# Routing inside the output projection, expert rows added in DRAM by an accumulating DMA, and twelve raw weight pieces

## The reference

```python
x = x + jnp.concatenate([o_diff, o_swa], axis=-1) @ w_out[l]
n2 = rms_norm(x, norm2_g[l])
x = x + hier_moe(n2, ...)          # top group of 4, then top 2 of its 8 experts
return rms_norm(x, final_g)

# in hier_moe, T = 2048 tokens, 32 experts
pg = jax.nn.softmax(xt @ w_rg + b_rg);  p_top, g_idx = lax.top_k(pg, 1)
el = (xt @ w_re + b_re).reshape(T, N_GROUPS, EXPERTS_PER_GROUP)
v2, i2 = lax.top_k(take_along_axis(el, g_idx), 2)
gates = jax.nn.softmax(v2) * p_top
h = jax.nn.silu(xb @ w_gate[e]) * (xb @ w_up[e]);  y = h @ w_down[e]
out = out.at[token].add(y * gate)
```

## Time and profile before

| | us |
|---|---|
| median of 3 runs (2435.26 to 2440.82) | 2435.41 |
| span of the profiled execution | 2437.1 |
| `output_projection`, first residual to last | 1106.88 to 1327.22 |
| `routing`, SP's first issue to the next stage's | 1341.66 to 1405.48 |
| `experts`, first turning of x to last copy of y | 1412.87 to about 2345.8 |
| `combine`, first issue to the end | 2348.89 to 2437.1 |

### The profile page before, as it was taken

The page is one execution under the profiler, slowest core; times in us unless marked ns, Lnnn a source line. Parts: engine busy times, 40 slices in busy tenths (PEclk is TensorE's granted clock), DMA queues, the critical chain, the costliest instruction groups (busy, mean ns, idle before and its releaser), DMA issues. The chain is left out here.

```text
span 2437.1 us, 39765 instructions
## 1 busy us (share of the span) xinstructions
PE 2097.6 (86%) x12636; PEld 1764.5 (72%) x12637; DVE 1347.6 (55%) x2184; ACT 1114.7 (46%) x2349; POOL 427.7 (18%) x568
## 2 busy tenths in 40 slices
PE   5999999779999947969999278999999999999940
PEld 4888888657777737958787267888887888788840
DVE  5333332278888834642332867565467467655537
ACT  4111111167887834642322157555456456645512
POOL 0112111123333432001110300000000000000036
PEclk9999999989999978989999589999999999999975
DMA  6323323341243464333331379777679679877648
GB/s 195 105 89 105 97 91 96 100 141 54 78 138 108 131 168 117 90 91 104 103 103 69 108 251 346 259 271 254 223 267 319 218 256 333 277 248 258 215 150 298
DMA packets 333564, 421.86 MB, mean 173 GB/s; under 512 B 19761, under 2 KB 245681, under 8 KB 333489
## 3 DMA queue, kind: packets, MB, share of 16 engines
q1 hardware_dynamic: 313056, 349.80, 45.1%
q0 software_dynamic: 12672, 46.14, 5.7%
q10 hardware_dynamic: 7760, 24.97, 2.6%
HBM read 321.76 MB, written 99.09 MB: 173 GB/s over the span
## 5 line engine op out<-in xcount | busy, mean ns | idle before, releaser
L56 PE MATMUL proj<-w_in_lo,n1T_hi 128*128 128x512 f32 (+1 forms) x640 | 245.0, 383 | 18.1 <-DVE w_in_lo L257 18.1
L57 PE MATMUL proj<-w_in_hi,n1T_lo 128*128 128x512 f32 (+1 forms) x640 | 239.5, 374 | 0.0
L58 PE MATMUL proj<-w_in_hi,n1T_hi 128*128 128x512 f32 (+1 forms) x640 | 239.3, 374 | 0.0
L525 ACT ACTIVATE prob<-score,nmax 128x512 f32<-128x512 f32 (+3 forms) x344 | 206.5, 608 | 52.0 <-DVE nmax L599 47.5
L1694 DVE TENSOR_TENSOR wg_lo<-raw_pieces,wg_hi 128x1024 fp32r<-128x1024 f32 x124 | 146.9, 1222 | 118.5 <-ACT wg_hi L1662 118.3
L57 PE MATMUL u_ps<-wu_hi,xT_lo 128*128 128x256 f32 x752 | 211.3, 281 | 0.0
L58 PE MATMUL u_ps<-wu_hi,xT_hi 128*128 128x256 f32 x752 | 211.3, 281 | 0.0
L56 PE MATMUL u_ps<-wu_lo,xT_hi 128*128 128x256 f32 x752 | 211.2, 281 | 0.0
L561 POOL TENSOR_SCALAR prob<-prob,scale,lam 128x512 f32<-128x512 f32 (+3 forms) x172 | 147.1, 866 | 241.0 <-DVE scale L615 224.9
L599 DVE TENSOR_REDUCE nmax<-score 128x2 f32<-128x1024 f32 (+3 forms) x172 | 171.5, 997 | 26.6 <-PE score L639 18.0
L56 PE MATMUL y_ps<-wd_lo,hT_hi 128*128 128x512 f32 x376 | 157.8, 420 | 28.5 <-DVE hT_lo L1705 28.1
(11 more groups left out here) (236 smaller groups left out, 5015.8 us busy)
## 6 DMA issues: line engine op xcount, KB each, us to landing
raw_pieces<-in_w_gate SPq DMA_DIRECT2D x128, 512.0 KB, 6.0
raw_pieces<-in_w_up SPq DMA_DIRECT2D x128, 512.0 KB, 6.9
raw_pieces<-in_w_down SPq DMA_DIRECT2D x128, 512.0 KB, 4.8
qk_scratch<-qkT SPq DMA_DIRECT2D x96, 256.0 KB, 2.3
y_scratch<-y ACTq DMA_DIRECT2D x47, 512.0 KB, 6.8
x_sb<-in_x SPq DMA_DIRECT2D x32, 512.0 KB, 4.5
y_scratch<-zero SPq DMA_DIRECT2D x32, 512.0 KB, 4.0
q_swa<-qk_scratch SPq DMA_DIRECT2D x32, 256.0 KB, 4.2
```

What stands on the lines that cost most here:

```text
L56: pe.matmul(out, hi, w_lo, start=first, stop=False)
L57: pe.matmul(out, lo, w_hi, start=False, stop=False)
L58: return pe.matmul(out, hi, w_hi, start=False, stop=last)
L525: act.activation(prob[:, n % RING, c, 0:w], score[:, n % BUFS, c, 0:w], ACT.Exp, bias=nmax[:, c, n:n + 1], accum_out=part[:, c, n:n + 1]). ...
```

## The change

1. **`output_projection` also routes.** For tile t-2, DVE takes the logits, the best group, the masked expert logits, the two best experts and their one-hot rows (`choose`, 13 instructions), and for tile t-3 the ranks, the destination and the two gates (`place`, 7 instructions). PE counts with two small matmuls (`count`), ACT makes two exponentials (`gate_exps`), and POOL scatters (token, gate) pairs of 8 bytes into a table in DRAM, `slots_d`, two indirect DMAs for each tile. The loop is written out 16 times rather than run as a loop. The stage `routing` is gone, but a short `block_table` at the end remains.
2. **The residual goes to DRAM** (`acc_d`), stored by SP per tile ahead of the loads of tile t+2; `x` has a semaphore of its own and is loaded last. In tiles 0 to 7 (`EARLY = 8`) SP loads, ACT and DVE split one piece each of the first expert's gate and up weights.
3. **`experts`:** a block's tokens and gates are read from `slots_d` by a DMA of POOL ahead of the gather; ACT multiplies by the gate as it copies y; POOL adds y into `acc_d` by an accumulating indirect DMA and waits for it. `y_scratch` is gone, and so is ACT's store.
4. **Weights:** the raw buffers are 12 pieces, filled by six loads of 1 MB for each expert instead of twelve of 0.5 MB.
5. **`combine`** reads `acc_d` in six plain loads on SP, all issued at its start, squares, normalizes and stores; no gather and no adding.
6. The 32 stores of zeros to `y_scratch` in `diff_attention` become three stores; the identity matrix is loaded once.

```diff
 @block.gpsimd   # experts
-def gather(b):
+def gather(b, row):
     pool.wait_ge(x_turned, b + 1)
-    pool.tensor_copy(idx[:, :], slots[:, bass.ds(b, 1)]).then_inc(idx_ready, 1)
-    pool.wait_ge(idx_ready, b + 1)
+    pool.dma_start(slot[:, :], slots_d[bass.ds(row * P, P), :]).then_inc(slot_in, 16)
+    pool.wait_ge(slot_in, b * 16 + 16)
     pool.indirect_dma_start(x[:, :], None, n2_d, ...).then_inc(x_in, 16)
+def keep(b):
+    pool.wait_ge(x_in, b * 16 + 16)
+    pool.tensor_copy(own[:, 0:1].bitcast(I32), slot[:, 0:1].bitcast(I32)).then_inc(own_ready, 1)
+    pool.tensor_copy(own[:, 1:2], slot[:, 1:2]).then_inc(own_ready, 1)
+    pool.wait_ge(own_ready, b * 2 + 2)
-def one_block(b, e, replaced):
-    gather(b + 1)
+def one_block(b, e, replaced, row):
+    gather(b + 1, row)
+    pool.wait_ge(y_ready, b + 2)
+    pool.indirect_dma_start(acc_d, bass.IndirectOffsetOnAxis(ap=own[:, 0:1].bitcast(I32), axis=0),
+                            y[:, :], None, compute_op=ALU.add).then_inc(y_added, 16)
+    pool.wait_ge(y_added, b * 16 + 16)
+    keep(b + 1)
 @block.scalar   # experts
     act.wait_ge(y_done, b + 1)
-    act.wait_ge(y_stored, b * 16 + 16)
-    act.copy(y[:, :], y_ps[:, :, :].rearrange("p a b -> p (a b)")).then_inc(y_ready, 1)
-    act.wait_ge(y_ready, b + 2)
-    act.dma_start(y_d[bass.ds(b * P, P), :], y[:, :]).then_inc(y_stored, 16)
+    act.wait_ge(own_ready, b * 2 + 2)
+    act.activation(y[:, :], y_ps[:, :, :].rearrange("p a b -> p (a b)"), ACT.Copy,
+                   scale=own[:, 1:2]).then_inc(y_ready, 1)
 @block.sync     # experts
-    sp.wait_ge(*(lo_there(e + 1, k - RAW) if k >= RAW else lo_there(e, k - RAW + PIECES)))
-    load_piece(sp, (w_gate, w_up, w_down), raw, raw_in, e + 1, k)
+    sp.wait_ge(*lo_there(e, 2 * j + 1))
+    load(e + 1, j)
 @block.vector   # output_projection, per tile
     residual(t, s)
     low_o(t + 1, 1 - s)
     normalize(t, s)
     sub_norm(t + 2, s)
     low_swa(t + 2, s)
-    take_logits(t - 1, 1 - s)
+    if 1 <= t <= EARLY:
+        low_w(t - 1)
+    if t >= 2:
+        choose(t - 2, s)
+    if t >= 3:
+        place(t - 3, 1 - s)
 @block.sync     # output_projection, per tile
     sp.wait_ge(h_ready, t + 1)
+    sp.dma_start(acc_d[t * P:(t + 1) * P, :], h[:, s, :]).then_inc(h_stored[s], 16)
     load(t + 2, s)
+    if t < EARLY:
+        load_w(t)
     sp.wait_ge(n2_ready, t + 1)
     sp.dma_start(n2_d[t * P:(t + 1) * P, :], n2[:, s, :]).then_inc(stored[s], 16)
+    sp.wait_ge(h_stored[s], 16 * (t // 2 + 1))
+    load_x(t + 2, s)
 @block.sync     # combine
+for b, (first, last) in enumerate([(0, 1), (1, 2), (2, 4), (4, 8), (8, 12), (12, 16)]):
+    sp.dma_start(acc[:, first:last, :], acc_d[first * P:last * P, :]...).then_inc(acc_in[b], 16)
```

More of the change, by code:

```diff
@@ L1204, in tile @@
                         .then_inc(rstd_ready, 1)
-                    if not (static(t) and t >= TILES - 2):
+                    if t + 2 < TILES:
                         sub_root(t + 2, s)
-                sub_root(0, 0)
-                sub_root(1, 1)
-                over_pairs(pool, tile)
+                    if t >= 4:
+                        scatter(t - 4)
+                for t in range(LAST - 3, TILES):
+                    scatter(t)
+                pool.wait_ge(scattered, 16 * TOPK * TILES)
+                pool.sem_inc(placed, 1)
             @block.tensor
@@ L1268 @@
+                pe.wait_ge(place_step, LAST * PLACE + 1)
+                for last, a in ((False, before), (True, both)):
+                    mm = pe.matmul(count_ps, a[:, LAST % 2, :], ones[:, 0:1], start=not last, stop=last)
+                mm.then_inc(total_pe, 1)
+                pe.wait_ge(total_step, 3)
+                pe.matmul(start_ps, nb[0:E, :], tri[0:E, 0:E + 1], start=True, stop=True).then_inc(total_pe, 1)
+MAX_TOK = 1e30
 BLOCKS = 64
-MAX_TOK = 1e30
 FF = 512
@@ L1517, in experts @@
-def experts(nc, sem, n2_d, w_gate, w_up, w_down, ident_d, wg, wu, raw, raw_in, hi_ready, lo_ready, slots, starts,
-            ends, y_d):
-    SIGNALLED = [0, 1, 2, 4, 6, 8, 9, 10]
-    with ExitStack() as ctx:
-        def sb(name, shape, dt=F32):
-            return ctx.enter_context(nc.sbuf_tensor(name, shape, dt))
-        def ps(name, shape):
-            return ctx.enter_context(nc.psum_tensor(name, shape, F32))
-        ident = sb("ident6", [P, P])
+        raw = sb("raw_pieces", [P, PIECES, PW])
@@ L1876, in tile @@
-                def tile(t, s):
-                    if not (static(t) and t >= TILES - AHEAD):
-                        gather(t + AHEAD, (s + AHEAD) % RING)
-                    b = s % 2
+                for t in range(TILES):
                     pool.wait_ge(ss_ready, t + 1)
-                    pool.tensor_tensor(var[:, b:b + 1], ss[:, b:b + 1], power[:, 1:2], ALU.add).then_inc(var_ready, 1)
+                    pool.tensor_tensor(var[:, t:t + 1], ss[:, t:t + 1], power[:, 1:2], ALU.add).then_inc(var_ready, 1)
@@ L1902, in _ @@
-                over_rings(act, tile)
+                for t in range(TILES):
+                    for b, (first, _) in enumerate(BATCHES):
+                        if t == first:
+                            act.wait_ge(acc_in[b], 16)
+                    if t >= 2:
+                        act.wait_ge(ss_ready, t - 1)
+                    act.activation(sq[:, t % 2, :], acc[:, t, :], ACT.Square, scale=1.0 / math.sqrt(D),
+                                   accum_out=ss[:, t:t + 1]).then_inc(ss_ready, 1)
@@ L1904, in _ @@
             @block.vector
             def _(dve):
-                def normalize(t, b):
+                dve.wait_ge(const_in, 16)
+                for t in range(TILES):
                     dve.wait_ge(rstd_ready, t + 1)
-                    if not (static(t) and t < 2):
-                        dve.wait_ge(stored[b], (t - b) * 8)
-                    dve.scalar_tensor_tensor(out=o[:, b, :], in0=acc[:, b, :], scalar=rstd[:, b:b + 1],
+                    dve.scalar_tensor_tensor(out=o[:, t, :], in0=acc[:, t, :], scalar=rstd[:, t:t + 1],
@@ L1964, in build @@
-                output_projection(nc, sem, x, o_d, mix_d, wo_hi, wo_lo, wo_split, subln_g, norm2_g, w_router_group,
-                                  b_router_group, w_router_expert, b_router_expert, ident, h_sb, logits, n2_d)
-            wg = [sb(f"wg_{part}", [P, KD, FF], F32R) for part in ("hi", "lo")]
-            wu = [sb(f"wu_{part}", [P, KD, FF], F32R) for part in ("hi", "lo")]
-            raw = sb("raw_pieces", [P, RAW, PW])
-            raw_in = [sem(f"raw_in{r}") for r in range(RAW)]
@@ L1971, in build @@
-            hi_ready = sem("hi_ready")
-            lo_ready = sem("lo_ready")
-            routing(nc, sem, logits, tables, gates, dest, slots, starts, ends, (w_gate, w_up, w_down), wg, wu, raw,
-                    raw_in, hi_ready, lo_ready)
-        experts(nc, sem, n2_d, w_gate, w_up, w_down, ident, wg, wu, raw, raw_in, hi_ready, lo_ready, slots,
-                starts, ends, y_d)
-        combine(nc, sem, y_d, final_g, h_sb, gates, dest, out)
+                window_attention(nc, sem, qk_d, v_d, sinks, ident_sb, band, mix_d, w_out, wo_hi, wo_lo, wo_raw, wo_split)
@@ new lines, in kept @@
+                def kept(name, shape, dt=F32):
+                    return held.enter_context(nc.sbuf_tensor(name, shape, dt))
+                starts = kept("starts", [1, N_EXPERTS + 1], I32)
+                ends = kept("ends", [1, N_EXPERTS], I32)
+                hi_ready, lo_ready = sem("w_hi_ready"), sem("w_lo_ready")
+                wg = [kept(f"wg_{part}", [P, KD, FF], F32R) for part in ("hi", "lo")]
+                wu = [kept(f"wu_{part}", [P, KD, FF], F32R) for part in ("hi", "lo")]
@@ L1980, in constants @@
+        combine(nc, sem, acc_d, final_g, power, out)
 def constants():
@@ L1999, in constants @@
         "tables": np.stack(tables).astype(np.float32),
+        "empty": empty,
     }
```

830 lines of the change are left out of this document (399 added, 431 removed).

## The result

| | before | after |
|---|---|---|
| median, us | 2437.36 (2435.26 to 2440.82, 4 runs) | 2882.22 (2872.55 to 2890.3, 4 runs) |
| ratio, 95% interval | | 1.1808 (1.1782 to 1.1833) |
| span of the profiled execution | 2437.1 | 2888.5 |
| last residual to first turning of x | 85.6 | 47.2 |
| `experts`, first turning of x to the last | 924.8 | 1449.1 |

The changed kernel is 18% slower. 2770 us were forecast, with 2480 to 2980 as the range. The difference of the spans, 451.4 us, is the sum of the rows' differences, rounded: -1.1 (last residual, 1326.16 instead of 1327.22), -38.4, +524.3, +9.6 and -42.9.

The account below looks back on a forecast made before the run. PE was taken to bound `experts`, with POOL's serial chain making it wait after the change. From 2437.1 us, +377 and +6 in `experts`, +28 `output_projection`, -45 `routing`, -32 `combine` gave 2771, forecast 2770 us, range 2480 to 2980.

Parts of the forecast that it names:

- The chain: `experts`: POOL's serial work from y ready to the next turning of x takes 16.9 us, with 10.2 us to hide it.
- The adding DMA: `experts`: adding y into DRAM takes 7.0 us, between bounds of 2.6 and 11.6.
- The loop's head: `experts`: POOL's loop head with its registers takes 0.4 us a block, between 0 and 1.
- The clock: `experts`: PE's wait lets the TensorE clock fall to 0.5 in the down product, 2.7 us in every block.
- The end of the stage: End of `experts`: last y, adding DMA, `keep` and barrier take about 9 us instead of 3.1, +6 us.
- Twelve raw pieces bring nothing: `experts`: twelve raw pieces and 1 MB loads gain nothing, as loads have 9 us more than they need in 27.9 us blocks.
- `output_projection`, +28 us: DVE's row decides; tiles take 17.0 to 18.2 us against 15.0: +28 us, bounds 0 and +45.
- `routing`, -45 us: From last residual to first turning of x, 41 us instead of 86: -45 us, between -35 and -50.
- `combine`, -32 us: `combine` moves 17.3 MB and takes 56 us instead of 88.2: -32 us, between -25 and -36.
- the short chain: Rival, chance 0.10, in `experts`: chain 11.1 us, blocks of 19.4, clock stays; 2375 us in all, 2.5% faster.
- the middle case: Rival, chance 0.19, in `experts`: short DMAs under little traffic, chain 14.5 us, no clock fall; 2533 us in all.
- the long one: Rival, chance 0.13, in `experts`: adding DMA at its 11.6 us bound, chain 24.1, blocks of 37.1; about 3190 us.

Follow-up runs that it names:

- plain write: Changed kernel with the indirect DMA of y writing into acc_scratch instead of adding, all waits kept: 2793.77 us.
- third-load run: Changed kernel with a third awaited 512 KB load (x again, into an unread buffer) for tiles 11 to 15 of `output_projection`: 2902.92 us.
- lagging kernel: Changed kernel with POOL gathering x for block b+1 first, then adding y of block b-1, wait for the adding DMA kept: 2345.1 us.
- run with extra matmuls: Changed kernel with 36 matmuls of 128x512, result unread, ahead of each wait for x: 2858.49 us.

## Why the prediction was right, and where its terms were off

**The mechanism was right.** POOL's serial chain behind y was named as the limit, and both taking the adding DMA out of it (2345 us) and taking one term out of it (2761 us) shortened the blocks. PE's wait for x, put at 6.7 us a block, was 10.5, and not alike everywhere as forecast, but 5.0 to 16.9 us. The chain, mean of the changed kernel's 46 full rounds against the sum:

| | predicted | measured |
|---|---|---|
| y ready to adding DMA to POOL's copy | 0.8 + 7.0 | 0.84 + 9.67 |
| copies, loop head, start of the table read | 0.5 + 0.4 + 0.8 | 2.52 |
| table read, start of the gather | 2.3 + 0.8 | 3.60 |
| gather to turning | 4.3 | 4.27 |
| chain | 16.9 | 20.9 |
| turning to y's end, clock included | 8.3 + 2.7 | 10.21 |

**The adding DMA was taken 2.7 us too short.** I took the plain store's 6.8 us and argued that the thinner traffic would pay for the extra read. The plain write measured just that, 6.64 us, and the adding one 9.67: the extra read wasn't paid for. The value lay between my bounds, 2.6 and 11.6, but in their upper half. The step that failed is the set-off against lighter traffic: per microsecond there was less of it (167 instead of 260 GB/s), but at an expert's end the loads of 1 MB are issued in the very moment in which y is added. One number was taken for two kinds of round. In the 16 without that traffic the adding DMA took 6.3 us and the whole chain 16.3, less than the sum; in the 30 at an expert's end they took 11.5 and 23.4. That the plain write's 6.64 us met the 6.8 is luck of the same kind: it is the mean of 3.5 and 8.3.

**The loop's head was put at 0.4 us.** It costs little within an expert (1.3 us from the start of POOL's copies to the table read) and about 3 us from one expert to the next, where POOL loads two numbers from `starts` and `ends` ahead of its gather. The mean is 2.52 us for this step instead of 1.7. That it is these two loads is read from the kernel; no run leaves them out. The earlier trace rows couldn't show it: there these loads lay inside a wait of 16.5 us.

**The clock** was taken as 2.7 us in the down product and cost 10.2 - 8.3 = 1.9, and the earlier trace rows was the right row for it.

**The end of the stage:** +6 forecast, +9.6 measured, with the same adding DMA and loop head in it.

**Twelve raw pieces bring nothing:** wrong as far as the loads of 1 MB go, where room for twelve instead of six was worth 34 us in one run (26 between the profiled executions). I reckoned with the loads' mean rate over a block; but a piece freed late is loaded late, and with room for six ACT waits for raw weights even in blocks of 31 us. As the changed kernel has the twelve pieces, this term was hidden in its time and the sum didn't show it. Against the six pieces of 0.5 MB of the kernel before it wasn't tested.

**`output_projection`, +28 us:** wrong. The stage ended 1.1 us earlier; tiles took 15.2 to 16.6 us while a weight piece was split in each, and 14.0 to 14.6 in the four after that, against 15.0 before. The 20 small instructions took 3.7 us, not 4.5, and the step that failed is the 12.5 us that I left in place, for two reasons. First, it came from one tile, and that was the longest of 13; the mean of the earlier trace rows's stretch is 11.7 us, and this is a tile like most:

```profile
1195.02 1.22 DVE L1077 TENSOR_TENSOR h_sb<-proj,x_sb 128x1024 f32 x1 [0.41 <-issue]
1205.80 0.69 DVE L1108 TENSOR_TENSOR mixT_lo<-swaT,mixT_hi 128x512 fp32r<-128x512 f32 x1
```

Second, DVE's part got shorter, to 10.4 to 12.1 us, 10.9 on average. What changed there is that x is no longer among the awaited loads; "the two have the same size" overlooked that the store ahead of the loads has x's size, but nobody waits for its end. The third-load run shows that an awaited load has its price; it doesn't separate this cause of the 0.9 us from the others.

**`routing`, -45 us:** -38.4. 47.2 us instead of 41, since the first table read and gather took 13.8 us from POOL's issue of the read to the turning (1359.53 to 1373.32), not 10, and POOL's scatters ran until 1353.

**`combine`, -32 us:** -42.9. I took 295 to 351 GB/s from the stage as it was, with gathers; with plain loads it moved 385 GB/s with the DMA engines at 0.97.

The terms of `experts` and its end were 151 us too small, `output_projection` 29 too large, `routing` 7 too small, `combine` 11 too large: 118 in all, which is 2888.5 - 2771. The total came closer than its largest term because 33 us of the other terms' errors went against it; that is luck. The rivals fell: the short chain needed an adding DMA of 2.6 us, and no landing in `experts` was under 5.8; the middle case needed a chain of 14.5 us and a clock that stays, the long one a chain of 24.1. The fit of the Trainium skill (DMA: Bandwidth & Descriptors, "Anatomy of one DMA — SWDGE (gpsimd) path"), an estimate of 3.2 us for 512 KB, doesn't agree with the adding DMA's median of 9.9 us either.

What stays open: whether the gather behind the adding DMA is slowed by its place in the queue or by the shared engines, how the value of twelve raw pieces divides between depth and size of the loads, and what shortened DVE's part in `output_projection`.

## What to carry to other kernels

On an engine that issues DMAs, ask of each wait what stands behind it. A DMA that nobody needs soon, and the wait for its end, belong behind the gather that the next block needs; moving the addition one block later cost a few small buffers and was worth 537 us, more than making it a plain write (88) or taking the table read away altogether (121). Not waiting for it at all in the old place brought less than moving it (144 us), because the read behind it on the same queue landed only after it.

Count what is waited for, not only what is moved: an awaited load of 512 KB more cost 2.6 us a tile. Take a duration from several tiles, not from one; here the one was the longest. And take the price of a DMA from a row with the traffic that will be around it at that moment, not with the stage's mean: the same adding DMA took 6.3 us in one kind of round and 11.5 in the other.

## What the runs showed of the hardware

- An indirect adding DMA of 512 KB landed in 9.9 us (median), the same as a plain indirect write in 7.5. Up to POOL's next copy the adding one took 6.3 us in the rounds with under 1 MB of traffic beside it and 11.5 in those with 2.9 to 5.6 MB; the plain one 3.5 and 8.3. POOL's issue of it was busy for 2.57 us on average, up to 8.12, and for 1.15 as a plain write.
- A read of 1 KB in 128 rows landed in 2.0 us (median) on POOL's queue with no DMA ahead of it, in 7.3 behind an adding DMA on the same queue and always after it; on ACT's queue at the same moment it landed 4.4 us or more ahead of the adding one.
- The lagging kernel's gather took 7.7 us instead of 4.2 beside the adding DMA and 267 GB/s of traffic. PE waited for x ahead of only 6 of the 47 turnings behind the first, 24.6 us in all.
- A wait of at most 2.4 us ahead of the down product left the granted clock at 1.0 in 21 blocks of the run with extra matmuls. It fell to 0.5 in three with waits of 2.1 to 2.2 us and in all 22 with 2.8 us and more.
- POOL was idle for 2.7 to 2.8 us ahead of its next DMA where the kernel loads two numbers at the head of the loop over experts, and for 1.0 within an expert, without a releaser in the trace (`issue`, 91.6 us in 33 waits).
